# First projection half divided in the latent attention; last norm on tokens as partitions; first tail's closing norm in halves of token pairs

## The chip, the cores and the metric

The kernel runs on one core of a Trainium2 chip. The metric is the device time of one execution in microseconds. The kernel before has a median of 2648.96 us in 3 runs (2647.46 to 2650.83). One execution was profiled; it took 2648.21 us.

## What is computed

Two blocks run one after the other on one sequence of 512 tokens with 1024 features. The first block (a hybrid mixer and a mixture of experts) is not touched. The second block has two layers, each of a mixer and an MLP with residual sums and layer norms:

```python
x = layer_norm(ALPHA * x + (1 + gate_m) * (mixer(h) @ w), ln_mix_g, ln_mix_b)   # layer 0: latent attention, w = mla_w_o
h = x * (1 + scale) + shift                                              # of the next mixer or MLP
x = layer_norm(ALPHA * x + (1 + gate_f) * mlp(h), ln_ffn_g, ln_ffn_b)           # mlp: relu(h @ w1 + b1) ** 2 @ w2 + b2
```

`w1` is 1024 x 4096, `w2` 4096 x 1024. In layer 1 the mixer is S5, a state space model, whose first step is `u = h @ w_in` (1024 x 1024). The output is the x of layer 1, 512 x 1024 in f32.

## The kernel before, in words

The work is cut into stages. A stage holds one instruction stream for each engine, its instructions wait for each other by semaphores that are cleared at its start, and all engines meet between two stages. What follows a mixer in a layer is one stage, `tail_stage` (line 3734): layer 0 is **the first tail**, layer 1 **the second tail** (`last`). Before the first tail comes `latent_attention_stage` (line 3258); after it comes the stage `s5_in` (line 4995).

**Layout.** The activations are kept transposed: `k.x` is 128 partitions (features) by 8 **chunks** of 128 features by 512 tokens. A product in nearly full f32 is made of fp32r parts: ScalarE copies a tensor to its rounded **high** part (`high`), VectorE subtracts that from the tensor for the **low** part (`low`), and TensorE sums three products (high x high, high x low, low x high; `three`). To make both parts of a tensor is called **to divide** it here.

**Halves of weights.** The weights of a tail come in 36 pieces of 256 columns, called halves, numbered 0 to 35 and 1 MB each: 0 to 3 are the mixer's output projection, then come two steps with 8 halves of `w1` and 8 of `w2` each. `RES` is 4 and `EXTRA` is 5, the first two of `w1`; N is 36, so that N-2 and N-1 (34, 35) are the last two of `w2`. They give the chunks 6 and 7 of the MLP's output: 34 holds the first 1024 rows of the second step, 35 the other 1024, and both sum into the same PSUM banks. SP loads half n into one of four raw buffers once half n-4 is divided; the first four were asked for in the stage before. Each half is divided as a whole (128 x 2048) into one of two buffers; RES and EXTRA go to a free half of `big`. The order in which halves are divided is `ORDER`. A half is 2 output chunks x 8 input chunks x 3 products = 48 products of 512 columns. TensorE also runs **filler products** (`k.fill`) on unused data.

**The inner norm** of a tail (`HalvedNorm`, line 3609) follows the projection. VectorE **evicts** each output chunk from PSUM into `k.x` (`evict`: times gate plus residual). The sum of chunks 0 and 1 goes through a product with ones, the **shift product** (`pe_shift`), which gives a first guess of the mean; it is subtracted from each chunk (`dve_shift`), ScalarE squares, VectorE sums chunks and squares, and a second product with ones, the **sums** (`pe_sums`), gives mean and variance in every partition. Half 3 and all that follows the sums run in two token halves of 256, so that TensorE makes the second token half of half 3 while the first is normalised. Then each chunk is centred, scaled, given its weights by ScalarE and divided, chunk by chunk, while TensorE already multiplies chunk after chunk with RES and EXTRA.

**The closing norm** (`TokenNorm`, line 3484) has the same steps on all 512 tokens after half 35. In the first tail its result feeds the first half of the S5 projection (`ahead`, class `S5Input`, line 4949), which TensorE runs at the end of the tail: 8 chunks x 4 values of l x 3 products, where the weight operand holds every fourth token (`x[:, a, kk, l::4]`). The projection's weights are loaded and divided in four **parts**: 0 and 1 are the first column half, 2 and 3 the second. In the second tail TensorE transposes each normalised chunk (4 transposes of 128 x 128), ScalarE copies it out of PSUM, and SP stores it (8 stores of 256 KB).

**Beside it** (`beside`), the first tail prepares S5 parameters, on ScalarE and VectorE between other work; their loads are the first of the stage in SP's queue.

Of the kernel before, what the change touches and what calls it, by code (L numbers as in the profile page):

```python
# [3257 lines left out]
def latent_attention_stage(k, cq, ckv, k_pe, cos, sin, o_parts, ahead):  # L3258
# [9 lines left out]
    with k.stage("latent_attention", "w_loaded0", "w_loaded1", "qp_done", "qn_done", "kn_done", "v_done", "qn_copied", "kn_copied", "v_copied", "rope_step",  # L3268
                 "rotated", "scores_done", "masked", "max_done", "exp_done", "inverted", "probs_done", "turned", "turned_copied", "weighed", "o_high",
                 "o_low") as (block, s, sb):  # L3270
# [15 lines left out]
        def _(pe):  # L3286
# [78 lines left out]
            weigh(last - 1)  # L3365

        @block.scalar
        def _(act):
# [39 lines left out]
            for g in range(last):  # L3408
# [200 lines left out]
class HalvedNorm:  # L3609
# [10 lines left out]
    LATE_BANK = 3  # L3620

    def __init__(self, k, s, name, sq, d_sum, q_sum):
# [4 lines left out]
        self.s = {x: s[f"{name}_{x}"] for x in self.SEMS}  # L3627

# [13 lines left out]
    def pe_sums(self, pe, h):  # L3642
        s, ones, t = self.s, self.k.ones[:], token_half(h)
        pe.wait_ge(s["d_added"], self.at(KD - 1, h))
        pe.matmul(self.mean[h], ones, self.d_sum[:, t], start=True, stop=True).then_inc(s["mean_done"], 1)
        pe.wait_ge(s["q_added"], self.at(KD - 1, h))
        pe.matmul(self.var[h], ones, self.q_sum[:, t], start=True, stop=True).then_inc(s["var_done"], 1)

    def act_square(self, act, c, h=None):
        s, t = self.s, slice(0, T) if h is None else token_half(h)  # L3650
# [3 lines left out]
        act.activation(self.sq[:, c % 2, t], self.x[:, c, t], ACT.Square).then_inc(s["squared"], 1)  # L3654

    def act_spread(self, act, h):
        s = self.s
        act.wait_ge(s["mean_done"], h + 1)
        act.activation(self.d_sum[:, token_half(h)], self.mean[h], ACT.Square, scale=1.0 / D).then_inc(s["spread"], 1)

    def act_root(self, act, h):
        s, rstd = self.s, self.q_sum[:, token_half(h)]
# [8 lines left out]
    def dve_shift(self, dve, c, h=None):  # L3671
        s, t = self.s, slice(0, T) if h is None else token_half(h)
        x = self.x[:, c, t]
        if c == 0:
            dve.wait_ge(s["shift_done"], 1)
        dve.scalar_tensor_tensor(out=x, in0=self.shift[:, t], scalar=-1.0 / self.FIRST, in1=x, op0=ALU.mult, op1=ALU.add).then_inc(s["shifted"], 1)  # L3676

    def dve_add(self, dve, c, h=None):

        s, t = self.s, slice(0, T) if h is None else token_half(h)  # L3680
        at = self.at(c, h or 0)
# [3 lines left out]
        before = self.x[:, 0, t] if c == 1 else self.d_sum[:, t]  # L3685
        dve.tensor_tensor(self.d_sum[:, t], before, self.x[:, c, t], ALU.add).then_inc(s["d_added"], 1)  # L3686

    def dve_add_square(self, dve, c, h=None):
        s, t = self.s, slice(0, T) if h is None else token_half(h)
        at = self.at(c, h or 0)  # L3690
# [3 lines left out]
        before = self.sq[:, 0, t] if c == 1 else self.q_sum[:, t]  # L3694
        dve.tensor_tensor(self.q_sum[:, t], before, self.sq[:, c % 2, t], ALU.add).then_inc(s["q_added"], 1)  # L3695

    def dve_pair(self, dve, p):

        if p == 0:
            self.dve_sum(dve)  # L3700
            return
        mine = range(0 if p == 1 else 2 * p, 2 * p + 2)
# [9 lines left out]
    def dve_centre(self, dve, c, h):  # L3712
        s, x = self.s, self.x[:, c, token_half(h)]
# [4 lines left out]
    def dve_var(self, dve, h):  # L3718
        s, t = self.s, token_half(h)
        dve.wait_ge(s["spread"], h + 1)  # L3720
        dve.wait_ge(s["var_done"], h + 1)
        dve.scalar_tensor_tensor(out=self.q_sum[:, t], in0=self.var[h], scalar=1.0 / D, in1=self.d_sum[:, t], op0=ALU.mult,
                                 op1=ALU.subtract).then_inc(s["var_ready"], 1)

    def dve_scale(self, dve, c, h):
        s, t = self.s, token_half(h)
        x = self.x[:, c, t]
# [3 lines left out]
        dve.tensor_tensor(x, x, self.q_sum[:, t], ALU.mult).then_inc(s["normed"], 1)  # L3731


def tail_stage(k, layer, w_mix, x_parts, big, divided, out=None, ahead=None, beside=None):
# [18 lines left out]
    norm_sems = [f"{a}_{x}" for a, norm in (("mix", HalvedNorm), ("ffn", TokenNorm)) for x in norm.SEMS]  # L3753
    SUMS_AT, LATE_SUMS_AT = 5, 4
    with k.stage(name, "high_done", "low_done", "tile_done", "cols_step", "x_scaled", "evicted", "h_done", "x_high", "x_low", "x_ready",
# [1397 lines left out]
```

## Time and profile before

| | |
|---|---|
| median of 3 runs | 2648.96 us |
| profiled execution | 2648.21 us, span 2646.4 us |
| mean granted TensorE clock | 0.973 |
| PE (TensorE products) | 2495.6 us, 94% of the span |
| PEld (TensorE weight loads, beside the products) | 1997.6 us, 75% |
| DVE (VectorE) | 1741.0 us, 66% |
| ACT (ScalarE) | 1149.3 us, 43% |
| POOL (GpSimd) | 63.2 us, 2% |

Times in rows count from the start of the span. A timeline row gives the start, the time from the first instruction of the group to its end, the engine, the line of the code, the operation, output and inputs with their shapes, the count, and in square brackets the idle time before it with what ended it. The latent attention ends at about 1592 us of the span, the first tail at 2038.6, and the second tail runs from about 2217 to the end.

### The profile page before, as it was taken

What the parts mean: (1) busy time and instruction counts of PE and PEld (TensorE: products, weight loads), DVE (VectorE), ACT (ScalarE), POOL (GpSimd) and SP (SyncE); (2) the same over time, 40 slices, a digit from 0 to 9 for tenths busy, and PEclk for the clock granted to TensorE, in tenths of its full rate; (3) what the DMA queues carried; (4) which work ended last, traced back from release to release, by engine and by line L of the source; (5) the groups of instructions that cost most, each with busy time, mean ns of one, the idle gap of its engine ahead of it and who ended that gap; (6) DMA issues with size and microseconds to landing.
All of it is one profiled execution on the core that took longest, in us unless ns stands there. A gap on an engine that the chain in (4) does not pass through costs nothing. (4 is left out here: it accounts for less than half of the span.)

```text
span 2646.4 us, 34407 instructions
## 1 busy us (share of the span) xinstructions
PE 2495.6 (94%) x13529; PEld 1997.6 (75%) x13529; DVE 1741.0 (66%) x2582; ACT 1149.3 (43%) x1683; POOL 63.2 (2%) x166
## 2 busy tenths in 40 slices
PE   7999999999999999899998898999999889999999
PEld 5666678777777878788875457888888877888887
DVE  4899545588775666899965566677765764732435
ACT  5444422255554225588853344622324244531323
POOL 0000000000000000100001000000000000000000
PEclk9999999999999988999999999999999899999999
DMA  7887727233335733899972213234331413233221
GB/s 264 263 286 267 250 82 283 85 104 92 84 104 176 257 78 155 341 420 421 416 277 95 62 42 104 80 120 135 112 112 62 142 64 135 82 103 96 96 80 32
DMA packets 299505, 427.49 MB, mean 162 GB/s; under 512 B 27690, under 2 KB 213533, under 8 KB 289488
## 3 DMA queue, kind: packets, MB, share of 16 engines
q1 hardware_dynamic: 289424, 395.13, 43.3%
q0 software_dynamic: 5392, 20.97, 2.0%
q10 hardware_dynamic: 4528, 9.18, 0.9%
q8 instruction: 108, 1.77, 0.3%
q14 instruction: 53, 0.43, 0.0%
HBM read 384.11 MB, written 41.14 MB: 161 GB/s over the span
## 5 line engine op out<-in xcount | busy, mean ns | idle before, releaser
L3864 PE MATMUL banks<-big,late_parts 128*128 128x512 f32 (+1 forms) x2016 | 445.6, 383 | 5.9 <-PEq L151 3.8
L3864 PEld LDWEIGHTS banks<-big,late_parts 128*128 128x128 f32 x2016 | 369.5, 190 | 80.8 <-issue 6.1
L3864 PE MATMUL banks<-h_parts_second,late_parts 128*128 128x512 f32 x1344 | 305.3, 389 | 0.0
L3864 PEld LDWEIGHTS banks<-h_parts_second,late_parts 128*128 128x128 f32 x1344 | 252.2, 188 | 52.2
L4080 DVE TENSOR_TENSOR late_parts<-w_second,late_parts 128x2048 fp32r<-128x2048 f32 x67 | 153.5, 2292 | 193.1 <-ACT late_parts L3948 193.0
L2379 DVE TENSOR_TENSOR expert_parts<-w,expert_parts 128x2048 fp32r<-128x2048 f32 x102 | 232.6, 2288 | 21.7 <-ACT expert_parts L2375 20.7
L3948 ACT ACTIVATE late_parts<-w_second 128x2048 fp32r<-128x2048 f32 x67 | 128.2, 1914 | 241.8 <-PE banks L3864 241.7
L1344 PE MATMUL banks<-h_parts,ssm_parts 128*128 128x512 f32 x960 | 231.3, 398 | 0.8 <-DVE ssm_parts L1611 0.4
L2375 ACT ACTIVATE expert_parts<-w 128x2048 fp32r<-128x2048 f32 x102 | 194.7, 1916 | 60.8 <-PE banks L2386 54.2
L1344 PEld LDWEIGHTS banks<-h_parts,ssm_parts 128*128 128x128 f32 x960 | 180.3, 190 | 44.1 <-issue 6.9
L2386 PE MATMUL banks<-expert_parts,expert_xt 128*128 128x512 f32 x816 | 192.2, 395 | 4.1 <-DVE expert_xt L2367 4.1
L2386 PEld LDWEIGHTS banks<-expert_parts,expert_xt 128*128 128x128 f32 x816 | 153.5, 190 | 36.7 <-DVE expert_xt L2367 4.8
L881 PE MATMUL banks<-h_parts,front_parts 128*128 128x512 f32 x552 | 137.8, 400 | 0.0
L551 PE MATMUL banks<-h_parts,front_parts 128*128 128x512 f32 x576 | 132.2, 391 | 2.7 <-PEq L151 2.7
L551 PEld LDWEIGHTS banks<-h_parts,front_parts 128*128 128x128 f32 x576 | 108.0, 188 | 26.4 <-issue 4.2
L3982 ACT ACTIVATE tail_r<-banks,cols 128x512 f32<-128x512 f32 x64 | 40.5, 685 | 183.3 <-PE banks L3864 183.3
L551 PE MATMUL banks<-h_parts,ssm_parts 128*128 128x512 f32 x480 | 111.5, 394 | 5.9 <-DVE h_parts L1965 3.1
L881 PEld LDWEIGHTS banks<-h_parts,front_parts 128*128 128x128 f32 x552 | 101.7, 191 | 19.7
L1134 DVE SCALAR_TENSOR_TENSOR attention_mod_sum<-w,silu_c,attention_mod_sum 128x512 f32<-128x512 f32 x147 | 110.4, 751 | 4.5
L551 PEld LDWEIGHTS banks<-h_parts,ssm_parts 128*128 128x128 f32 x480 | 91.0, 190 | 26.1 <-issue 3.9
L4160 DVE TENSOR_TENSOR tail_q<-tail_r 128x512 f32<-128x512 f32 x64 | 41.4, 688 | 97.2 <-ACT tail_r L3982 97.1
L2386 PE MATMUL banks<-expert_parts,expert_ht 128*128 128x512 f32 x408 | 98.9, 399 | 3.0 <-ACT experts_y L2879 3.0
(726 smaller groups left out, 3914.1 us busy)
## 6 DMA issues: line engine op xcount, KB each, us to landing
w_second<-in_mlp_w_dram SPq DMA_DIRECT2D x64, 1024.0 KB, 5.1
w<-in_w_exp_gate_dram SPq DMA_DIRECT2D x34, 1024.0 KB, 9.0
w<-in_w_exp_up_dram SPq DMA_DIRECT2D x34, 1024.0 KB, 8.6
w<-in_w_exp_down_dram SPq DMA_DIRECT2D x34, 1024.0 KB, 8.8
w<-in_w_in_dram SPq DMA_DIRECT2D x64, 512.0 KB, 4.5
w<-in_mod_mix_w_dram SPq DMA_DIRECT2D x24, 1024.0 KB, 5.1
w<-in_mod_ffn_w_dram SPq DMA_DIRECT2D x23, 1024.0 KB, 6.1
w<-in_w_in_dram SPq DMA_DIRECT2D x16, 1024.0 KB, 5.5
```

Source lines behind the costliest of these rows:

```text
L551: mm = pe.matmul(out, self.parts[:, n % 2, w, kk, f * P:(f + 1) * P], x[:, v, kk, :], start=(start and kk == 0 and j == 0), stop=(stop and ...
L881: mm = pe.matmul(ps[:, bank, :], parts[:, j, w, kk, :], k.hp[:, x, kk, :], start=(kk == 0 and n == 0), stop=(kk == KD - 1 and n == 2))
L1134: ins = dve.scalar_tensor_tensor(out=acc, in0=w, scalar=by, in1=acc, op0=ALU.mult, op1=ALU.add)
L1344: mm = pe.matmul(ps[:, t % 2, :], parts[:, t % SPLITS, w, kk, :], k.hp[:, x, kk, :], start=(kk == 0 and j == 0), stop=(kk == KD - 1 and j ...
L2375: act.activation(self.high_part(h), self.raw(h), ACT.Copy).then_inc(self.high_done, 1)
L2379: dve.tensor_tensor(self.low_part(h), self.raw(h), self.high_part(h).bitcast(F32), ALU.subtract).then_inc(self.low_done, 1)
L2386: mm = pe.matmul(out, x[:, v, first + kk, :], self.tile(h, w, kk), start=(start and kk == 0 and j == 0), stop=(stop and kk == KE - 1 and j ...
L3864: mm = pe.matmul(ps[:, bank(n, f), t] if out is None else out, w_part(n, w)[:, kk, f * P:(f + 1) * P], x[:, v, kk, t], start=(first_chunk( ...
L3948: act.activation(w_part(n, 0), raw_half(k, n), ACT.Copy).then_inc(s["high_done"], 1)
L3982: act.activation(r[:, c % 2, :], ps[:, bank(n, c % HT), :], ACT.Relu, bias=k.cols[:, b1 + at:b1 + at + 1]).then_inc(s["relu_done"], 1)
L4080: dve.tensor_tensor(w_part(n, 1), raw_half(k, n), w_part(n, 0).bitcast(F32), ALU.subtract).then_inc(s["low_done"], 1)
L4160: dve.tensor_tensor(q[:, c % 2, :], r[:, c % 2, :], r[:, c % 2, :], ALU.mult).then_inc(s["squared"], 1)
```

## The change

It has three parts.

**Projection and inner norm.** Half 0 of `mla_w_o` is divided in the latent attention stage (ScalarE and VectorE, between the heads' last steps) into a free part of `big`; the filler products move from the start of the first tail to the end of the attention's TensorE stream. In the first tail `ORDER` becomes 0, 1, 2, RES, EXTRA, 3. In both tails the shift product stands between the two output chunks of half 1, the weight copy of half 6 two chunks later, and VectorE's order around it is new.

**Closing norm of the first tail** (`PairedNorm`). Halves 34 and 35 and all that follows are run in two halves of tokens, each of which holds two neighbouring tokens of every four (256 columns as 128 pairs). The S5 projection starts with l = 0 and 1 on the first half. Part 1 of its weights is divided by GpSimd instead of VectorE.

**Closing norm of the second tail** (`ClosingNorm`). Halves 34 and 35 run in two token halves. TensorE transposes the shifted chunks between the products of these halves, and ScalarE copies them to `by_token` (tokens as partitions). The sums are products with a single column of ones, so that mean and deviation are one number per partition. Two VectorE operations on 128 x 1024 finish a block of 128 tokens (`weigh`, `finish`); for block 0 GpSimd does the second. Four stores of 512 KB follow. The rows of weight and bias of the norm are loaded to all partitions at the start of the stage, ahead of the weights in SP's queue.

```diff
+            k.fill(pe, ps[:, 7, 0:P], 14)
...
+                if g == last - 4:
+                    act.wait_ge(k.raw_loaded[0], 16 * (k.raw_base[0] + 1))
+                    act.activation(room[0], raw_half(k, 0), ACT.Copy).then_inc(s["w_high"], 1)
...
+                if g + 2 == last:
+                    dve.wait_ge(s["w_high"], 1)
+                    dve.tensor_tensor(room[1], raw_half(k, 0), room[0].bitcast(F32), ALU.subtract).then_inc(s["w_low"], 1)
...
+class PairedNorm(HalvedNorm):
...
+    SPREAD_AFTER = "var_done"
...
+    def pick(self, ap, h):
+        if h is None:
+            return ap
+        return ap.rearrange("p (j l) -> p j l", l=S5_HALF)[:, :, h * (S5_HALF // 2):(h + 1) * (S5_HALF // 2)]
...
+class ClosingNorm(HalvedNorm):
...
+    def pe_sums(self, pe, h):
+        s, one = self.s, self.k.ones[:, 0:1]
+        for which, (total, added, done) in enumerate(((self.d_sum, "d_added", "mean_done"), (self.q_sum, "q_added", "var_done"))):
+            pe.wait_ge(s[added], self.at(KD - 1, h))
+            for j in range(self.BLOCKS):
+                b = h * self.BLOCKS + j
+                mm = pe.matmul(self.sums_of(h, which)[:, j:j + 1], total[:, b * P:(b + 1) * P], one, start=True, stop=True)
+            mm.then_inc(s[done], 1)
...
+    def dve_stats(self, dve, h, step):
+        s, b = self.s, self.blocks(h)
+        dve.wait_ge(s["mean_done"], h + 1)
+        dve.wait_ge(s["var_done"], h + 1)
+        step(dve.tensor_scalar(self.stats[:, 0, b], self.sums_of(h, 0), 1.0 / D, None, ALU.mult))
+        step(dve.tensor_tensor(self.stats[:, 1, b], self.stats[:, 0, b], self.stats[:, 0, b], ALU.mult))
+        dve.scalar_tensor_tensor(out=self.stats[:, 2, b], in0=self.sums_of(h, 1), scalar=1.0 / D, in1=self.stats[:, 1, b], op0=ALU.mult,
+                                 op1=ALU.subtract).then_inc(s["var_ready"], 1)
...
-        ORDER = (0, 1, RES, EXTRA, 2, 3, *range(EXTRA + 1, N))
+        extra = [half_room(big, j) for j in range(2)]
...
+        ORDER = (0, 1, *((RES, EXTRA, 2) if last else (2, RES, EXTRA)), 3, *range(EXTRA + 1, N))
...
+        in_extra = {RES: 0, EXTRA: 1} if last else {0: 0, RES: 1, EXTRA: 0}
...
+            if last:
+                for j, row in enumerate(("ln_ffn_g_2", "ln_ffn_b_2")):
+                    sp.dma_start(out_rows[:, j, :], k.ins[row][layer:layer + 1, :].to_broadcast([P, D])).then_inc(s["rows_loaded"], 16)
...
+                for b in range(TB):
+                    if b == 0:
+                        sp.wait_ge(s["out_pool"], 2)
+                    else:
+                        sp.wait_ge(s["out_ready"], b)
+                    sp.dma_start(out[0, b * P:(b + 1) * P, :], y[:, b, :]).then_inc(s["stored"], 16)
+                sp.wait_ge(s["stored"], 16 * TB)
...
+                pool.wait_ge(s["next_high"], 2)
+                ahead.low(pool, 1, s["next_pool"])
+            else:
+                pool.wait_ge(s["weighed"], 1)
+                pool.wait_ge(ffn_norm.s["root_done"], 1)
+                pool.tensor_scalar(y[:, 0, :], y[:, 0, :], ffn_norm.scalar(2, 0), None, ALU.mult).then_inc(s["out_pool"], 1)
+                pool.wait_ge(s["out_pool"], 1)
+                pool.tensor_tensor(y[:, 0, :], y[:, 0, :], out_rows[:, 1, :], ALU.add).then_inc(s["out_pool"], 1)
...
-            if not split:
-                k.fill(pe, ps[:, 0, 0:P], 14)
+                    if f == 0 and between is not None:
+                        between(pe)
...
+            def closing_products(n, x):
+                pe.wait_ge(s["low_done"], place[n] + 1)
+                final = n == N - 1
+                for h in range(2):
+                    for f in range(HT):
+                        if n == N - 2 and h == 1:
+                            pe.wait_ge(s["added"], KD + (4 + 2 * f if last else 4))
+                        for kk in range(KD):
+                            mm = three(n, f, kk, x, ffn_norm.late(KD - 2 + f, h), lambda ap: ffn_norm.pick(ap, h))
+                            if final and h == 1 and f == 0 and kk == SUMS_AT:
+                                if last:
+                                    for c in (KD - 2, KD - 1):
+                                        ffn_norm.pe_turn(pe, c, s["turned"], s["out_copied"], 0)
+                                ffn_norm.pe_sums(pe, 0)
+                        if h == 1:
+                            mm.then_inc(s["tile_done"], 1)
+                        elif final:
+                            mm.then_inc(ffn_norm.s["early_done"], 1)
+                        if last and n == N - 2:
+                            for c in ((0, 1), (2,), (3, 4), (5,))[2 * h + f]:
+                                ffn_norm.pe_turn(pe, c, s["turned"], s["out_copied"])
...
+                products(n, x_parts, between=mix_norm.pe_shift if n == 1 else None)
...
+                pe.wait_ge(s["next_low"], 1)
+                for h in range(2):
+                    for kk in range(KD):
+                        if h == 0 and kk == ahead.HK:
+                            pe.wait_ge(s["next_pool"], 1)
+                        pe.wait_ge(s["x_low"], 2 * KD + KD * h + kk + 1)
+                        for l in range(h * (S5_HALF // 2), (h + 1) * (S5_HALF // 2)):
+                            ahead.products(pe, 0, l, kk)
+                        if h == 0 and kk == LATE_SUMS_AT:
+                            ffn_norm.pe_sums(pe, 1)
...
+            for j in range(2, 6):
+                high(ORDER[j])
+                if j >= 4:
+                    mix_norm.act_square(act, 2 * (j - 4))
+                    mix_norm.act_square(act, 2 * (j - 4) + 1)
...
+            halves_to_parts(mix_norm, H_SCALE, 0, lambda: high(EXTRA + 1))
...
+                            ffn_norm.act_square(act, c)
+                elif last and n == N - 2:
+                    for c in range(KD - 2):
+                        ffn_norm.act_copy(act, c, s["turned"], s["out_copied"])
...
-                turned_out(KD - 1)
+                for h in range(2):
+                    for c in (KD - 2, KD - 1):
+                        ffn_norm.act_square(act, c, h)
+                    for c in (KD - 2, KD - 1):
+                        ffn_norm.act_copy(act, c, s["turned"], s["out_copied"], h)
+                    ffn_norm.act_root(act, h)
...
+            def close():
+                closing = Steps(dve, s["closing_step"])
+                dve.wait_ge(s["rows_loaded"], 32)
+                for c in (KD - 2, KD - 1):
+                    add_and_sum(c, 0)
+                ffn_norm.dve_stats(dve, 0, closing)
+                weigh(0)
+                weigh(1)
+                add_and_sum(KD - 2, 1)
+                add_and_sum(KD - 1, 1)
+                finish(1)
+                ffn_norm.dve_stats(dve, 1, closing)
+                weigh(2)
+                weigh(3)
+                finish(2)
+                finish(3)
...
+            dve.sem_inc(s["low_done"], 1)
...
                 for c in range(2 * n, 2 * n + 2):
...
-                        evict_half(c, 0)
-                        mix_norm.dve_add(dve, c, 0)
-                        mix_norm.dve_add_square(dve, c, 0)
-                if n < RES - 1:
-                    mix_norm.dve_pair(dve, n)
-            normalise_halves()
+                    evict(c)
+                if n == 0:
+                    mix_norm.dve_sum(dve)
+                if n < 2:
+                    low(ORDER[4 + n])
+                mix_norm.dve_pair(dve, n)
...
+                        else:
+                            dve.wait_ge(s["next_high"], 1)
+                            ahead.low(dve, 0, s["next_low"])
+                            for c in (KD - 2, KD - 1):
+                                add_and_sum(c, 0)
+                            beside.beside(n)
+                            normalise_halves(ffn_norm, 2 * KD, add_half)
```

## Rows read from the trace of the kernel before

**Rows 1.** windows: busy us (instructions) by engine, clock, DMA; second tail's start and middle
```profile
2217.00:2242.00 25.00, 24.18 (x96) 19.81 (x97) 11.68 (x8) 14.44 (x13) 1.49 (x7) 0.88 0.40 126
...
2300.00:2400.00 100.00, 100.00 (x443) 82.84 (x442) 41.72 (x40) 38.29 (x44) 0.00 (x0) 1.00 0.30 96
```

**Rows 2.** timeline: start, us, engine, line, idle before; end of attention, start of first tail
```profile
1591.04 0.69 DVE L3449 CAST big<-banks 128x512 fp32r<-128x512 f32 x1 [2.59 <-PE banks L3338]
...
1592.78 3.36 PE L158 MATMUL banks<-ident 128*128 128x128 f32 x28 [1.77 <-PEq L151]
...
1598.33 23.64 PE L3864 MATMUL banks<-big,late_parts 128*128 128x512 f32 x96 [2.19 <-DVE late_parts L4080]
...
1600.26 84.25 SPq L3819 DMA_DIRECT2D w_second<-in_mlp_w_dram  x8
...
1606.83 1.92 ACT L3948 ACTIVATE big<-w_second 128x2048 fp32r<-128x2048 f32 x1 [4.92 <-DMA w_second<-in_mlp_w_dram]
```

**Rows 3.** timeline: first tail's inner norm and the products behind it
```profile
1644.01 0.70 PE L3645 MATMUL banks<-tail_sums,ones 128*128 128x256 f32 x2 [2.34 <-DVE tail_sums L3686]
...
1648.89 6.30 PE L3864 MATMUL banks<-h_parts_second,big 128*128 128x256 f32 x48 [0.16 <-DVE h_parts_second L4102]
...
1671.04 2.28 DVE L4080 TENSOR_TENSOR late_parts<-w_second,late_parts 128x2048 fp32r<-128x2048 f32 x1
```

**Rows 4.** timeline: second tail's start, inner norm and the products behind it
```profile
2217.82 24.54 PE L3864 MATMUL banks<-big,late_parts 128*128 128x512 f32 x96 [3.76 <-PEq L151]
...
2237.29 0.69 DVE L3669 TENSOR_TENSOR tail_sums<-x 128x512 f32<-128x512 f32 x1
...
2264.39 1.22 PE L3645 MATMUL banks<-tail_sums,ones 128*128 128x256 f32 x2 [2.34 <-DVE tail_sums L3686]
...
2270.40 7.64 PE L3864 MATMUL banks<-h_parts_second,big 128*128 128x256 f32 x60
...
2287.36 8.90 PE L3864 MATMUL banks<-h_parts_second,big 128*128 128x256 f32 x72 [0.55 <-DVE h_parts_second L4102]
```

**Rows 5.** timeline: first tail's last halves, its closing norm, the next stage
```profile
1980.97 1.92 ACT L3948 ACTIVATE late_parts<-w_second 128x2048 fp32r<-128x2048 f32 x1 [8.54 <-PE banks L3864]
...
2014.16 24.45 PE L4978 MATMUL banks<-big,h_parts_second 128*128 128x512 f32 x96 [2.36 <-DVE h_parts_second L4151]
...
2025.80 4.49 DVE L4987 TENSOR_TENSOR big<-w_second,big 128x2048 fp32r<-128x2048 f32 x2 [1.12 <-ACT big L4984]
...
2038.91 2.54 PE L4473 MATMUL banks<-ident,w_second 128*64 128x128 f32 x32 [0.30 <-PEq L151]
```

**Rows 6.** timeline: second tail's last halves and closing transposes
```profile
2601.94 1.92 ACT L3948 ACTIVATE late_parts<-w_second 128x2048 fp32r<-128x2048 f32 x1 [8.62 <-PE banks L3864]
...
2633.55 0.42 PEld L3939 LDWEIGHTS banks<-ident,x 128*128 128x128 f32 x4 [0.97 <-ACT x L4059]
```

**Rows 7.** timeline: a GpSimd addition beside a VectorE one
```profile
744.51 1.29 POOL L1330 TENSOR_TENSOR ssm_sq<-ssm_sq 128x512 f32<-128x512 f32 x1 [61.12 <-ACT ssm_sq L1545]
...
744.67 1.55 DVE L1715 TENSOR_TENSOR x<-x,ssm_parts_plain 128x384 f32<-128x384 f32 x1
```

**Rows 8.** lines by form, 1650 to 2647 us: busy us, mean ns, idle before
```profile
L3864 PEld LDWEIGHTS banks<-h_parts_second,late_parts 128*128 128x128 f32 x1344 | 252.2, 188 | 52.2
...
L4978 PEld LDWEIGHTS banks<-big,h_parts_second 128*128 128x128 f32 x192 | 46.1, 311 | 3.4 <-issue 2.7
...
L4742 ACT ACTIVATE h_parts_second_plain<-banks 128x256 f32<-128x256 f32 x16 | 8.2, 673 | 2.0 <-PE banks L4671 2.0
...
L3731 DVE TENSOR_TENSOR x<-x,tail_sums 128x256 f32<-128x256 f32 x29 | 12.1, 418 | 0.1
...
L4639 PEld LDWEIGHTS banks<-x,big_plain 64*64 64x64 f32 x384 | 11.5, 133 | 2.0 <-issue 1.0 <-ACT x L4722 1.0
...
L4656 PEld LDWEIGHTS banks<-big_plain,x 64*64 64x64 f32 x96 | 5.9, 136 | 0.2 <-issue 0.2
```

**Rows 9.** DMA issues: size of each, median us to landing
```profile
s_rotations<-s_room SPq DMA_DIRECT2D x4, 512.0 KB, 3.0
```

More of the change, by code:

```diff
@@ L3255, in width, with half_room, latent_attention_stage @@
         return (g % TB + 1) * P
-def latent_attention_stage(k, cq, ckv, k_pe, cos, sin, o_parts, ahead):
+def half_room(big, j):
+    return [big[:, v, KD + j * KD // 2:KD + (j + 1) * KD // 2, :].rearrange("p c t -> p (c t)").rearrange("p (k n) -> p k n", k=KD) for v in range(2)]
+def latent_attention_stage(k, cq, ckv, k_pe, cos, sin, o_parts, ahead, room):
     ps = k.ps
@@ L3620 @@
     LATE_BANK = 3
+    SPREAD_AFTER = "mean_done"
     def __init__(self, k, s, name, sq, d_sum, q_sum):
@@ L3770, in tail_stage @@
             k.raw_base[slot] += N // 4
-        split = 1 if last else 0
         b1 = k.places["mlp_b1_2"][0] + layer * K2
@@ L3789, in w_part, with used_before @@
         def w_part(n, j):
-            if n in (RES, EXTRA):
-                return extra[n - RES][:, j].rearrange("p c t -> p (c t)").rearrange("p (k n) -> p k n", k=KD)
-            return parts[:, n % 2, j]
+            kind, slot = room_of(n)
+            return extra[slot][j] if kind == "extra" else parts[:, slot, j]
+        def used_before(n):
+            return max((m for m in range(n) if room_of(m) == room_of(n)), default=None)
         def bank(n, f):
@@ L3872, in last_chunk, with products @@
                 return n < RES + UP or of(n)[1] < UP or (of(n)[1] - UP) % 2 == 1
-            def products(n, x):
-                if n >= split:
+            def products(n, x, between=None):
+                if n >= 1:
                     pe.wait_ge(s["low_done"], place[n] + 1)
@@ L3920, in _ @@
                     pe.wait_ge(s["relu_done"], HK * i + HT * (g + 5))
+                    if n >= N - 2:
+                        closing_products(n, hidden[:, :, chunk * KD:(chunk + 1) * KD, :])
+                        continue
                     products(n, hidden[:, :, chunk * KD:(chunk + 1) * KD, :])
@@ L3968, in half_affine, with halves_to_parts @@
                 act.wait_ge(s["h_done"], i + 1)
-                act.activation(h_parts[:, 0, c, t], q_half(i), ACT.Copy).then_inc(s["x_high"], 1)
+                act.activation(norm.pick(h_parts[:, 0, c], h), q_half(norm, i), ACT.Copy).then_inc(s["x_high"], 1)
+            def halves_to_parts(norm, at, before, between):
+                for c in (KD - 2, KD - 1):
+                    norm.act_square(act, c, 0)
+                norm.act_spread(act, 0)
+                norm.act_root(act, 0)
+                for c in range(KD):
+                    half_affine(c, 0, norm, at, before)
+                    if c == 4:
+                        norm.act_square(act, KD - 2, 1)
+                        norm.act_square(act, KD - 1, 1)
+                    if c == 6:
+                        norm.act_spread(act, 1)
+                norm.act_root(act, 1)
+                for c in range(KD):
+                    half_affine(c, 1, norm, at, before)
+                    if c == 3:
+                        between()
@@ L4131, in normalise_halves @@
                     if c >= 1:
-                        half_low(c - 1, 1)
-                half_low(KD - 1, 1)
+                        half_low(c - 1, 1, norm, before)
+                half_low(KD - 1, 1, norm, before)
             def add(n):
```

348 lines of the change are left out of this document (169 added, 179 removed).

## The prediction

> **What bounds the kernel now.** I read the page's busy times first (in the table above): TensorE is busy nearly all the span. The windows say what that means inside a tail: in 100 us of its middle TensorE has no free time, 443 products of 512 columns at full clock, 0.2257 us each [rows 1]. So nothing that VectorE, ScalarE or the queues do there is worth anything; the change can only give or take time where TensorE stands, and costs where it gives TensorE more to do. I then read the timeline at the four places the diff touches. The reader is to see four gaps. At the start of the first tail TensorE waits from 1591.04 to 1598.33 [rows 2]. In the inner norm of each tail it stands 2.34 us for the sums [rows 3, 4]. Between the first tail's last half and the S5 projection lies some 11 us: halves 34 and 35 begin at 1980.9 (when ScalarE sees half 33 done) and need 96 x 0.2257 = 21.7 us, to 2002.6; the projection's first product starts at 2014.16 [rows 5]. After the last product of the second tail comes a closing chain of VectorE, ScalarE, transposes and stores: from half 33's end (2601.9) [rows 6] to the span's end, 2646.4, are 44.5 us, of which 21.7 are products.
>
> After a gap TensorE also runs slower for a while: the 96 products behind the 3.76 us gap took 24.54 us instead of 21.67 [rows 4], in a stretch whose mean granted clock is 0.88, so part of it at 1.2 instead of 2.4 GHz [rows 1]. The same 96 cost 23.64 behind 2.19 us of idle [rows 2] and 24.45 behind 2.36 us [rows 5]. I price a gap above 2 us at 2.0 to 2.9 us on top of itself.
>
> **Term 1, start and inner norm of the first tail.** Half 0 of the projection is divided in the attention stage; its VectorE subtraction (2.25 us, half of 4.49 [rows 5]) fits the 2.59 us for which VectorE waits there anyway [rows 2], the ScalarE copy lies in similar waits. If that cover were gone, the hand-over would slip by up to 2.25 us. But the filler products (3.36 us) now stand ahead of the stage's end instead of behind it. A stage begins 0.30 us after its last engine ended (2014.16 + 24.45 = 2038.61, next 2038.91 [rows 5]), so the tail begins at 1591.04 + 3.36 + 0.30 = 1594.7, not 1592.78; products start 3.6 us earlier than 1598.33.
> This does not last. The shift product now stands in the middle of half 1, after 72 products, at 1594.7 + 16.25 = 1610.95. It needs the sum of two evicted chunks, and VectorE evicts only after dividing halves 1, 2 and 4 (`for n in ORDER[1:4]: low(n)`). Half 4's load is queued on SP behind the S5 parameter loads, 7.5 us after the stage began, and ScalarE's copy waited for it until 1606.83, 14.05 us after [rows 2]. Again 14.05 us: 1608.75; copy 1.92, subtraction 2.25, two evictions and a sum, about 0.7 each: 1615.0. So TensorE stands 4.1 us at a place where it did not stand before; behind the waiting product are queued the second chunk of half 1 and halves 2 and 3, and VectorE's eviction of chunk 3 waits for these. Half 4's load no longer waits for half 0's subtraction, but SP is not free sooner. With 0.9 for the shift and 24 products (5.4), half 1 ends at 1621.4, plus 2.0 to 2.9 for the clock, say 1623.8; before, 1598.33 + 23.64 + 0.9 = 1622.9. The early start is lost: 0.9 us later.
> Then the reordering pays: chunk 0 and 1 are shifted, summed and squared before half 1 ends. Counting VectorE's operations from there (half 3's subtraction, chunks 2 to 5, two half chunks) the sums are ready 19.3 us after it, about when TensorE arrives; before they were ready after 21.1 (1644.01 - 1622.9) [rows 3]. Gain 1.8. The weight copy that stood between the second and third chunk of the second token half moves two chunks on and its 0.55 us stall (seen in the twin [rows 4]) goes. Term 1: -0.9 + 1.8 + 0.55 = 1.5 gained. Bounds: -0.5 (the clock lost for longer) and 3.9 (clock kept).
>
> **Term 2, inner norm of the second tail.** Here halves 4 and 5 come in time: the sum began at 2237.29 and was ready at 2238.0 [rows 4], behind the subtractions of four halves; half 2's (2.25) now stands behind it, so 2235.7, and TensorE arrives at 2236.9 (2217.82 + 24.54 - 5.4) [rows 4]. No stall. The same 1.8 to 2.0 us, and the slow clock behind the stall (6.0 us from the sums to the products at 2270.40 against 4.9 in the twin, 1644.01 to 1648.89 [rows 3, 4]), 1.1, and 0.55: 3.5 us. Two broadcast row loads now stand ahead of the weights on SP; at worst they cost the 1.2 us of slack and a stall. I take 3.3, bounds 1.4 and 3.6.
>
> **Term 3, the first tail's closing norm.** Halves 34 and 35 run as 256 columns: 192 products instead of 96. 48 took 6.30 us, 72 took 8.90 [rows 3, 4]: 0.131 and 0.124, I take 0.127. Half 34: 12.2 instead of 10.8. ScalarE divides two S5 parts after it (3.8 us), VectorE the first of them, to 16.6 (all from 1980.9), and GpSimd the second, 128 x 2048. GpSimd's 128 x 512 addition took 1.29 us; four times that is 5.2, to 21.8. Beside that addition a VectorE operation on 384 columns took 1.55 us and ended when GpSimd's end (745.80) had left it its own 0.4 [rows 7]: an operation that reads two SBUF tensors waits for GpSimd. The sums of the first late chunk are such, so they wait to 21.8. (The Trainium skill, GPSIMD Engine Reference, section Elementwise — side-by-side cycle accounting, gives 4.50 us for an addition of this size; by that the term would be 0.7 us better.) With the second chunk (four operations of about 0.42 [rows 8], plus one left of the first) the sums are complete at 24.2, not at 20.8 where TensorE arrives. From the sums to the last subtraction of the normalised chunks the inner norm took 1644.01 to 1671.04, less 1.92 for the copy in it, 25.1 us [rows 3]; 0.6 more since the square now waits for the variance product. Then two more copies and two subtractions of S5 weights, which were hidden before, 6.4 us (1.9 + 4.49 [rows 5]): 56.3. TensorE's 96 products end about 2 us before that, so VectorE ends the stage; TensorE's new wait for GpSimd's half of the weights falls at about 35 and is long met. Before: 2038.61 - 1980.9 = 57.7. Term 3: 1.4 gained. Without GpSimd's hold, 3.2 more: 4.6. Dearer pair operands on ScalarE: a copy that writes every eighth element took 0.67 us for 256 [rows 8] against about 0.4; were half of that 0.27 paid on pairs, 32 operations would cost some 3.2 us: -1.8.
>
> **How pairs of tokens are read.** A weight load that takes every fourth element took 311 ns against 188 packed; one that takes every second, 136 against 133 [rows 8]. So I price pairs (two of four) at nothing on TensorE. The Trainium skill, Advanced Engine Details and Errata (section SBUF Cachelines), says both that two accesses to a 16-byte line are enough to hide the memory's latency and that a new line at each access costs something; by the first clause the sum stands, by a charge for each new line it would move towards rival 1. The row at every second element bears out the first; no row shows the moving operand in pairs.
>
> **Term 4, the second tail's closing norm.** From 2601.9 [rows 6]: half 34 12.2, six chunks of four transposes at 0.105 [rows 6] 2.5, a wait of 1.4 for ScalarE's first copy (it comes after half 35's copy and subtraction, two additions, a shift and two squares, at 7.7, and takes 0.6; TensorE is there at 7.0): 16.1. Half 35 to the sums: 48 + 18 products, 8.4, transposes and sums 1.4: 25.9. Three small operations, then two 128 x 1024 operations of 1.2 (between 0.42 for 256 and 2.25 for 2048 columns [rows 5, 8]): 29.0. GpSimd's block 0, 1.1 + 2.6, holds up the sums of the last two half chunks as in term 3: 35.0, not 32.6. Then 1.2, sums and scalars 0.5, four operations of 1.16: 41.4. The last store is now 512 KB, like one that took 3.0 [rows 9], and 0.3 for the end: 44.7 against 44.5. Term 4: -0.2. Bounds: 2.2 (GpSimd not in the way) and -1.5 (half of the remaining waits between engines longer).
>
> **Sum.** 1.5 + 3.3 + 1.4 - 0.2 = 6.0 us off the profiled execution's 2648.21 (1.8 around its span): 2642.2. That execution is 0.75 below the median, 2648.96; I put the time between both levels, **2642.5 us**.
>
> **Rivals.** (1) Slower: pairs are dear as TensorE's moving operand. Place: the 192 products of term 3. From 32 ns more each the whole gain is gone (6.0 / 192). At half of the 311 - 188 = 123 ns per 128 columns, over 256 columns 123 ns, it is 23.6 us: 2666. For it: the 311. Against: the 136. (2) GpSimd holds nothing up: 3.2 + 2.4 more gained, 2636.9. Against it stands the 1.55 us. (3) No stall at the moved shift, or the clock kept: 2.4 more, 2640.1; it needs half 4's load earlier, which nothing brings. (4) Pairs dear on ScalarE and VectorE alone: 2645.7.
>
> **How the numbers follow.** Forecast 0.50, rival 1 0.07, 2 0.15, 3 0.10, 4 0.18. A measurement of this kernel can tell about 0.2%, 5.3 us: faster means under 2643.7. The forecast, with about 2.5 us either way, lies there for two thirds, rivals 2 and 3 wholly, 4 for a tenth: 0.57. Slower (over 2654.3) is rival 1 and a rest of mishaps: 0.09. Same: 0.34. The range goes from 2636 (rival 2) to 2654, which leaves rival 1 out.
>
> **What would show it.** Right: TensorE idle about 4 us in the middle of half 1 of the first tail, no idle before the inner sums of either, VectorE operations beside GpSimd's 128 x 2048 one stretched, VectorE last before the S5 stage. Wrong: 256-column products above 0.15 us in half 34 of the first tail (rival 1); GpSimd's operation over before 2000 or VectorE unhindered beside it (rival 2); half 1 without a gap (rival 3); ScalarE's operations on 256 columns in pairs above 0.5 (copy) and 0.7 us (rival 4).

## The result, and the profile after

The changed kernel is slower by 0.3%: median 2656.56 us in 11 runs against 2648.04 us in 11, ratio 1.0028, 95% interval 1.0017 to 1.0038. Forecast were 2642.5 us and a range of 2636 to 2654.

The two profiles (spans 2646.4 and 2654.3 us) are compared stretch by stretch. The first fence shows the ends of stretches in the kernel before that no group above has; the second the timeline of the changed kernel, first tail (columns as in the rows above).

```profile
1675.14 45.07 PE L3864 MATMUL banks<-h_parts_second,late_parts 128*128 128x512 f32 x198
...
2296.10 24.22 PE L3864 MATMUL banks<-h_parts_second,late_parts 128*128 128x512 f32 x106
```

```profile
1592.53 0.69 DVE L3458 CAST big<-banks 128x512 fp32r<-128x512 f32 x1 [0.39 <-PE banks L3343]
...
1595.92 11.16 PE L4008 MATMUL banks<-big 128*128 128x512 f32 x48 [0.30 <-PEq L151]
1606.92 5.60 PE L4008 MATMUL banks<-big,late_parts 128*128 128x512 f32 x24
...
1611.28 1.91 ACT L4113 ACTIVATE big<-w_second 128x2048 fp32r<-128x2048 f32 x1 [6.21 <-DMA w_second<-in_mlp_w_dram]
...
1617.74 2.08 PE L3657 MATMUL banks<-tail_sums,ones 128*128 128x512 f32 x2 [5.22 <-DVE tail_sums L3686]
...
1644.99 0.70 PE L3662 MATMUL banks<-tail_sums,ones 128*128 128x256 f32 x2 [0.24 <-DVE tail_sums L3701]
...
1674.90 45.30 PE L4008 MATMUL banks<-h_parts_second,late_parts 128*128 128x512 f32 x199
...
1980.73 1.91 ACT L4113 ACTIVATE late_parts<-w_second 128x2048 fp32r<-128x2048 f32 x1 [8.96 <-PE banks L4008]
...
2006.62 4.86 POOL L5169 TENSOR_TENSOR big<-w_second,big 128x2048 fp32r<-128x2048 f32 x1 [405.11 <-ACT big L5166]
...
2009.25 2.52 DVE L3701 TENSOR_TENSOR tail_sums<-tail_sums,x 128x256 f32<-128x256 f32 x1
...
2017.71 0.63 PE L3662 MATMUL banks<-tail_sums,ones 128*128 128x256 f32 x2
...
2051.95 2.54 PE L4655 MATMUL banks<-ident,w_second 128*64 128x128 f32 x32 [1.37 <-PEq L151]
```

The reader is to see the new wait of 5.22 us at the moved shift product, almost none before the inner sums, and at the end no wait at all before the sums at 2017.71, though they come 37.0 us after half 33's end (1980.73, where ScalarE, which waits for that half, starts its next copy): TensorE was busy all that time. The second tail of the changed kernel:

```profile
2230.34 19.02 PE L4008 MATMUL banks<-big,late_parts 128*128 128x512 f32 x72 [3.76 <-PEq L151]
2249.66 1.12 PE L3657 MATMUL banks<-tail_sums,ones 128*128 128x512 f32 x2 [0.29 <-DVE tail_sums L3686]
...
2305.20 15.15 PE L4008 MATMUL banks<-h_parts_second,late_parts 128*128 128x512 f32 x66
...
2611.04 1.91 ACT L4113 ACTIVATE late_parts<-w_second 128x2048 fp32r<-128x2048 f32 x1 [8.96 <-PE banks L4008]
...
2638.18 3.75 POOL L4000 TENSOR_SCALAR h_parts_second_plain<-h_parts_second_plain,tail_stats 128x1024 f32<-128x1024 f32 x1 [405.86 <-DVE h_parts_second_plain L4316]
...
2640.54 0.42 DVE L3709 TENSOR_TENSOR tail_sums<-tail_sums,tail_r 128x256 f32<-128x256 f32 x1
...
2642.01 2.47 POOL L4002 TENSOR_TENSOR h_parts_second_plain<-h_parts_second_plain,tail_out_rows 128x1024 f32<-128x1024 f32 x1
...
2642.30 2.46 DVE L3709 TENSOR_TENSOR tail_sums<-tail_sums,tail_r 128x256 f32<-128x256 f32 x1
```

From such rows, with [rows 2, 4, 5, 6] for before:

| stretch | before | after | gained | forecast |
|---|---|---|---|---|
| span's start to the last head's cast (1591.04, 1592.53) | 1591.04 | 1592.53 | -1.49 | 0 (half 0's division hidden) |
| to the first 512-column products of the first MLP (term 1) | 84.10 | 82.37 | 1.73 | 1.5 |
| to half 33's end | 305.83 | 305.83 | 0 | 0 |
| to the S5 stage's first product (term 3) | 57.94 | 71.22 | -13.28 | 1.4 |
| to the second tail's first product | 178.91 | 178.39 | 0.52 | not touched |
| to the first 512-column products of its MLP (term 2) | 78.28 | 74.86 | 3.42 | 3.3 |
| to half 33's end | 305.84 | 305.84 | 0 | 0 |
| to the span's end (term 4) | 44.46 | 43.26 | 1.20 | -0.2 |
| sum | 2646.4 | 2654.3 | -7.90 | |

The first stretch holds the division of half 0. It did not delay the hand-over: the last cast follows the one before it by 7.06 us in both kernels (from 1583.98 and 1585.47). The 1.49 us were lost earlier, and in the nine profiles below, whose attention stage is the same as the changed kernel's, the last cast lies anywhere from 1590.0 to 1594.5.

Terms 1, 2 and 4 came in at or above the forecast; term 3 is the loss. Its price is in the lines by form (count, busy us, mean ns of one) of the changed kernel, 1975 to 2060 us:

```profile
L4008 PE MATMUL banks<-big,late_parts 128*128 128x256 f32 x192 | 44.6, 413 | 0.0
...
L4008 PE MATMUL banks<-big,late_parts 128*128 128x512 f32 x25 | 5.8, 389 | 0.0
```

A product of 256 columns read in pairs holds TensorE for 44.6 / 192 = 0.232 us, as long as one of 512 packed columns (5.8 / 25 = 0.232). The clock is not the reason: the granted clock was 1.00 from 1981 to 2003 us (third number from the end of the row).

```profile
1981.00:2003.00 22.00, 22.00 (x98) 19.87 (x97) 7.58 (x9) 3.12 (x4) 0.00 (x0) 1.00 0.19 66
```

The second tail's 192 products of the same size read packed columns:

```profile
L4008 PE MATMUL banks<-big,late_parts 128*128 128x256 f32 x192 | 24.4, 285 | 0.0
```

That is 0.127 us each; the pairs cost 20.2 us of TensorE.

### The profile page after: what moved, and what is told of

Read it like the earlier page. It is cut to its first block and busy times, and to the rows that moved or that the text cites. A ratio compares the mean times of both kernels' runs of the same rounds, so it can differ in the third digit from the quotient of the medians.

```text
span 2654.3 us, 34754 instructions
## 1 busy us (share of the span) xinstructions
PE 2497.8 (94%) x13649; PEld 2010.7 (76%) x13649; DVE 1751.3 (66%) x2626; ACT 1149.9 (43%) x1701; POOL 74.8 (3%) x169
## 5 line engine op out<-in xcount | busy, mean ns | idle before, releaser
L4008 PE MATMUL banks<-big,late_parts 128*128 128x512 f32 (+1 forms) x2160 | 458.4, 375 | 3.8 <-PEq L151 3.8
L4008 PEld LDWEIGHTS banks<-big,late_parts 128*128 128x128 f32 x2160 | 386.7, 191 | 73.4 <-issue 6.6
L1344 PEld LDWEIGHTS banks<-h_parts,ssm_parts 128*128 128x128 f32 x960 | 178.4, 188 | 43.1 <-issue 6.5
```

The source lines that it names most:

```text
L1344: mm = pe.matmul(ps[:, t % 2, :], parts[:, t % SPLITS, w, kk, :], k.hp[:, x, kk, :], start=(kk == 0 and j == 0), stop=(kk == KD - 1 and j ...
L4008: mm = pe.matmul(pick(ps[:, bank(n, f), :]) if out is None else out, w_part(n, w)[:, kk, f * P:(f + 1) * P], pick(x[:, v, kk, :]), start=( ...
```

## The experiments

Nine kernels ran. Ratios are to the kernel before, run on the same chip. Three ran once only (eight ways to read, GpSimd out of the second tail's closing, steps of the weight operand) and are read from their profiles.

**Pair order.** The hidden activations of the first tail's second MLP step are stored with the tokens of the first half first, so that halves 34 and 35 read packed columns; VectorE puts the tokens back when it evicts.

```diff
+                    if i == STEPS - 1 and not last:
+                        dst, src = dst.rearrange("p (h j l) -> p h j l", h=2, l=2), src.rearrange("p (j h l) -> p h j l", h=2, l=2)
+                    act.activation(dst, src, ACT.Relu, ...
...
-                            mm = three(n, f, kk, x, ffn_norm.late(KD - 2 + f, h), lambda ap: ffn_norm.pick(ap, h))
+                            mm = three(n, f, kk, x, ffn_norm.late_flat(KD - 2 + f, h), lambda ap: ap[:, token_half(h)])
```

> The changed kernel, but the hidden activations of the first tail's second step are written in pair order, so that the products of halves 34 and 35 read 256 packed columns. Theory A (a product that reads its moving operand in pairs takes the time of 512 columns, 0.232 us instead of 0.127, and nothing else of part 3 is dear): the 192 products take 24.4 instead of 44.6 us; the sums then wait for VectorE behind GpSimd's subtraction, at 24.2 us after half 33's end instead of 37.0, so some 12.8 us of the 20.2 come back: ratio to the kernel before 0.998 (0.9972 to 0.9990). Theory B (pairs are dear on ScalarE and VectorE too, or the closing chain is longer for another reason): the sums come no earlier than 30 us after half 33's end, ratio above 1.000.

Measured: 2641.64 us, ratio 0.9965 (0.9952 to 0.9977). Its timeline:

```profile
1979.03 1.91 ACT L4119 ACTIVATE late_parts<-w_second 128x2048 fp32r<-128x2048 f32 x1 [8.96 <-PE banks L4014]
...
1994.35 4.84 POOL L5183 TENSOR_TENSOR big<-w_second,big 128x2048 fp32r<-128x2048 f32 x1 [394.15 <-ACT big L5180]
...
1995.15 0.42 DVE L3692 SCALAR_TENSOR_TENSOR x<-banks,x 128x256 f32<-128x256 f32 x1
1995.61 3.86 DVE L3701 TENSOR_TENSOR tail_sums<-tail_sums,x 128x256 f32<-128x256 f32 x1
...
2001.17 1.05 PE L3662 MATMUL banks<-tail_sums,ones 128*128 128x256 f32 x2 [2.81 <-DVE tail_sums L3701]
...
2034.54 2.54 PE L4669 MATMUL banks<-ident,w_second 128*64 128x128 f32 x32 [1.37 <-PEq L151]
```

The sums come 2001.17 - 1979.03 = 22.14 us after half 33's end, and the stretch of term 3 is 2034.54 - 1979.03 = 55.51 us instead of 71.22. Theory A holds, and theory B falls: with packed columns the paired norm is 2.4 us shorter than the old one, for 1.4 forecast, with GpSimd's hold and TensorE's wait for it in the trace. The ratio lies a little below A's range.

**Eight ways to read the moving operand**, in one kernel, each with a line of its own, such as

```diff
+            def every_second(n, f, kk, x, out, w, v, st, sp):
+                return pe.matmul(out, w_part(n, w)[:, kk, f * P:(f + 1) * P], x[:, v, kk, :].rearrange("p (j l) -> p j l", l=2)[:, :, 0], start=st, stop=sp)
```

> The changed kernel, with eight ways to read the moving operand in the closing products of the first tail (24 products each; other tokens than the norm's are read, so the output of chunks 6 and 7 is other than the reference's). If a product is paid by the 16-byte lines (four f32) that it reads, at 512 columns of 0.226 us in 128 lines: 256 packed columns 0.127 (64 lines), 4 of 8 aligned 0.127 (64 lines), 4 of 8 across lines 0.226 (128), 6 of 8 (252 columns, 84 lines) 0.15, 2 of 4 0.23 (128), 2 of 4 across lines 0.45 (254 lines), every second 0.23 (128 lines), every fourth (128 columns, 128 lines) 0.23. If instead any step that isn't packed halves the rate: 4 of 8 takes 0.23 like 2 of 4, every fourth 0.13, and across lines or not makes no difference.

Its timeline of TensorE; the difference of two starts over the count is the price of one:

```profile
1982.34 2.99 PE L4029 MATMUL banks<-big,late_parts 128*128 128x256 f32 x24
1985.17 5.60 PE L4032 MATMUL banks<-big,late_parts 128*128 128x256 f32 x24
1990.59 5.62 PE L4035 MATMUL banks<-big,late_parts 128*128 128x256 f32 x24
1996.03 3.06 PE L4050 MATMUL banks<-big,late_parts 128*128 128x256 f32 x24
1998.92 5.61 PE L4041 MATMUL banks<-big,late_parts 128*128 128x256 f32 x24
2004.35 5.63 PE L4044 MATMUL banks<-big,late_parts 128*128 128x254 f32 x24
2009.79 2.30 PE L4047 MATMUL banks<-big,late_parts 128*128 128x128 f32 x18
2011.91 0.63 PE L3662 MATMUL banks<-tail_sums,ones 128*128 128x256 f32 x2
...
2013.51 3.80 PE L4038 MATMUL banks<-big,late_parts 128*128 128x252 f32 x24
2017.15 8.02 PE L5192 MATMUL banks<-big,h_parts_second 128*128 128x512 f32 x30
```

In this order: 4 of 8 aligned 0.118, 4 of 8 across lines 0.226, every second 0.227, packed 0.120, 2 of 4 0.226, 2 of 4 across lines 0.227, every fourth (128 columns) 0.118, 6 of 8 (252 columns) 0.152. (By starts a product comes out a little shorter than by busy time over count, 0.226 and 0.120 for 0.232 and 0.127.) Both theories miss: the price by lines fails at 2 of 4 across lines (0.227, not 0.45) and every fourth (0.118, not 0.23), the price of any step fails at 4 of 8 aligned. One rule fits: a whole aligned group of four f32 goes at 0.46 ns a column (0.118 / 256), every other column at 0.88 to 0.89. For 6 of 8 that makes (4 x 0.46 + 2 x 0.88) / 6 x 252 = 0.151 us. Every fourth can't bear it out: its 128 columns took as long as 256 packed ones, but the 28 fillers of [rows 2], 128 packed columns each (in plain f32), took 3.36 / 28 = 0.120 us too, so 0.118 may be what a product of few columns takes anyway. The rule is read from the other seven, in one run; why the chip does so isn't shown.

**The old closing norm** in the first tail, the rest as changed:

```diff
-            ffn_norm = PairedNorm(k, s, "ffn", r, sums[:, 0, :], sums[:, 1, :])
+            ffn_norm = TokenNorm(k, s, "ffn", 4, r, sums[:, 0, :], sums[:, 1, :])
...
-                    if n >= N - 2:
+                    if n >= N - 2 and last:
```

> The changed kernel with the first tail's closing norm of the kernel before (halves 34 and 35 as products of 512 columns, norm on all tokens, both first parts of the S5 weights divided by VectorE). Theory A: the loss lies in part 3 alone, 13.3 us in the profiles; without it the time is 2643 us, ratio 0.9978 (0.9970 to 0.9986), the sum of the terms 1, 2 and 4. Theory B (the profiles mislead, the other parts gain nothing against the medians): ratio 0.9995 to 1.0005.

Measured: 2643.28 us, ratio 0.9976 (0.9966 to 0.9986). Theory A: the loss lies in "part 3", the stretch of term 3 (the second of the three parts of the change), alone, and terms 1, 2 and 4 together are worth the 6.35 us (0.24%) that the profiles say.

**Evictions first** in the first tail:

```diff
-            for n in ORDER[1:4]:
+            for n in ORDER[1:4 if last else 3]:
                 low(n)
...
                     mix_norm.dve_sum(dve)
+                    if not last:
+                        low(ORDER[3])
```

> The changed kernel, but in the first tail VectorE evicts chunks 0 and 1 and sums them before it divides half 4. Theory A (the 5.2 us stall at the moved shift product is VectorE waiting for half 4's load): the stall is gone, TensorE reaches the sums 5 to 7 us earlier and waits there up to 3 us for VectorE; 3 to 5 us faster than the changed kernel, ratio to the kernel before 1.0012 (1.0003 to 1.0020). Theory B (VectorE's work up to the sums is the bound): the wait moves to the sums whole, ratio 1.0028 as the changed kernel.

Measured: 2650.72 us, ratio 1.0004 (0.9994 to 1.0014), against 1.0028. Theory A, and more of it than expected. Its timeline of TensorE:

```profile
1597.89 11.16 PE L4008 MATMUL banks<-big 128*128 128x512 f32 x48 [0.30 <-PEq L151]
...
1614.33 1.02 PE L3657 MATMUL banks<-tail_sums,ones 128*128 128x512 f32 x2
...
1639.87 0.70 PE L3662 MATMUL banks<-tail_sums,ones 128*128 128x256 f32 x2 [0.24 <-DVE tail_sums L3701]
```

From the first product to the sums are 41.98 us, in the changed kernel 1644.99 - 1595.92 = 49.07: 7.1 us less, the wait of 5.22 and the clock behind it (granted 0.79 from 1617 to 1625 us in the changed kernel, so partly at 1.2 GHz; 1.00 here from 1614 to 1622). Nothing of it comes back at the sums. The two windows, the changed kernel's first:

```profile
1617.00:1625.00 8.00, 7.26 (x23) 5.25 (x24) 6.16 (x7) 1.23 (x2) 0.00 (x0) 0.79 0.00 1
...
1614.00:1622.00 8.00, 8.00 (x35) 6.26 (x34) 6.66 (x6) 4.19 (x5) 0.00 (x0) 1.00 0.50 177
```

**GpSimd out of the first tail's closing**, on top of pair order:

```diff
-                pool.wait_ge(s["next_high"], 2)
-                ahead.low(pool, 1, s["next_pool"])
...
+                            dve.wait_ge(s["next_high"], 2)
+                            ahead.low(dve, 1, s["next_pool"])
                             beside.beside(n)
```

> The kernel with pair order, but VectorE instead of GpSimd makes the low part of part 1 of the S5 weights, after its sums of the first half's late chunks. Theory A (GpSimd's 128 x 2048 subtraction held up VectorE's addition, 3.86 us instead of 0.42): the addition takes 0.42, TensorE waits at most 0.7 us for the sums instead of 2.81, and the S5 stage begins 53.2 us after half 33's end instead of 55.5, 2.3 us faster (ratio to the kernel before 0.9956). Theory B (the addition is slow for its own pairs): it still takes above 2 us, and the stage begins 55.5 us or more after half 33's end.

Measured: 2638.87 us, ratio 0.996 (0.9944 to 0.9975). By the medians that can't be told from pair order (0.9965); the timeline tells it:

```profile
1977.66 1.91 ACT L4117 ACTIVATE late_parts<-w_second 128x2048 fp32r<-128x2048 f32 x1 [8.96 <-PE banks L4012]
...
1994.24 0.43 DVE L3701 TENSOR_TENSOR tail_sums<-tail_sums,x 128x256 f32<-128x256 f32 x1
...
1996.83 0.62 PE L3662 MATMUL banks<-tail_sums,ones 128*128 128x256 f32 x2
...
2002.72 8.02 PE L5174 MATMUL banks<-big,h_parts_second 128*128 128x512 f32 x30 [1.22 <-DVE h_parts_second L4262]
...
2030.02 2.54 PE L4669 MATMUL banks<-ident,w_second 128*64 128x128 f32 x32 [1.36 <-PEq L151]
```

The same addition takes 0.43 us, TensorE doesn't wait for the sums (it waits 1.22 us later, for the first normalised chunk), and the stretch of term 3 is 52.36 us instead of 55.51. Theory A: GpSimd held VectorE up. (The Trainium skill, GPSIMD Engine Reference, section Key points, says that the two share their SBUF interfaces and contend where VectorE has two SBUF inputs; the 3.86 and 0.43 us agree. It was not so beside every operation of GpSimd: while it multiplied a tensor by a scalar for 3.75 us in the second tail of the changed kernel, VectorE's sums, with two SBUF inputs, took 0.42 to 0.43.)

**GpSimd out of the second tail's closing** (`finish(0)` on VectorE after `weigh(1)`):

> The changed kernel, but VectorE finishes block 0 of the output (one operation more of 1.2 us) and GpSimd does nothing in the second tail's closing. Theory A (GpSimd's 128 x 1024 addition held up VectorE's last sum, 2.46 us instead of 0.42): that sum takes 0.42, and the last store is issued 0.8 us earlier, at 2.05 saved less 1.2 added. Theory B (the hold cost nothing, since VectorE waited anyway): 1.2 us later.

In one run the last sum takes 0.42 us, and from half 33's end to the span's end are 42.88 us instead of 43.26:

```profile
2645.58 0.42 DVE L3709 TENSOR_TENSOR tail_sums<-tail_sums,tail_r 128x256 f32<-128x256 f32 x1
...
2647.59 0.16 DVE L3839 TENSOR_SCALAR tail_stats<-banks 128x2 f32<-128x2 f32 x1 [0.39 <-PE banks L3812]
```

The hold is real; only 0.4 of the 0.8 us expected shows, since VectorE now waits 0.39 us for TensorE's sums.

**All four edits:**

> The changed kernel with all four edits: pair order, VectorE's evictions before half 4 in the first tail, part 1's low part and block 0 on VectorE. If they add up, by the medians and profiles so far: 0.9965 less 0.0024, 0.0009 and 0.0003, ratio to the kernel before 0.993 (0.9915 to 0.9945). If the earlier start of the first tail is given back behind it (VectorE as the bound in both): 0.9955.

Measured: 2631.22 us, ratio 0.9929 (0.9916 to 0.9943). They add up.

**Steps of the weight operand**, for the row on which the prediction had rested:

```diff
+            elif l == 1:
+                mm = pe.matmul(out, x[:, a, kk, 0:256:2], moving, start=first, stop=final)
+            elif l == 2:
+                mm = pe.matmul(out, x[:, a, kk, 0:384:3], moving, start=first, stop=final)
```

> The changed kernel, with other steps of the weight operand in the second column half of the S5 projection (it reads other tokens there, so the output is another): every fourth as before for l = 0, every second for l = 1, every third for l = 2, packed for l = 3, each 24 loads of 128 x 128. Theory A (a weight load hides a step of two, and the moving operand does not: each has its own price): every second 190 to 200 ns like packed, and its product 0.23 us; every fourth 311. Theory B (a step of two is dear in a load of this size too, and the 136 ns row was of a smaller load that had slack): every second above 240 ns.

Its lines by form, weight loads (every fourth, third, second, packed):

```profile
L5162 PEld LDWEIGHTS banks<-big,h_parts_second 128*128 128x128 f32 x28 | 6.7, 310 | 0.0
...
L5166 PEld LDWEIGHTS banks<-big,h_parts_second 128*128 128x128 f32 x24 | 5.6, 253 | 0.2 <-issue 0.2
L5164 PEld LDWEIGHTS banks<-big,h_parts_second 128*128 128x128 f32 x24 | 4.6, 193 | 0.9
L5168 PEld LDWEIGHTS banks<-big,h_parts_second 128*128 128x128 f32 x24 | 4.5, 188 | 0.9
```

Theory A: a weight load takes a step of two for 5 ns, where the moving operand pays double. Pairs in a weight load were not measured.

**Evictions first in both tails**, on top of all four edits: `for n in ORDER[1:3]`, and `low(ORDER[3])` behind the sum in both.

> The kernel with all four edits, and VectorE's evictions before the second divided half of the MLP in the second tail as well. Theory A (in the second tail the shift product waited for the loads behind the two row loads, 1.55 us in the profile with all four edits): no wait there, 1.5 us faster, ratio to the kernel before 0.9923 (0.991 to 0.9938). Theory B: the wait moves to the sums, ratio 0.9929 as with four edits.

Measured: 2628.52 us, ratio 0.9925 (0.9911 to 0.9938), the lowest median of the nine. The wait at the second tail's shift product is gone (1.55 us in the profile with four edits); the ratio can't tell it from 0.9929.

## Why the prediction was wrong

The step that failed is the one on how pairs are read: "So I price pairs (two of four) at nothing on TensorE". It took the moving operand's price from weight loads, of which a step of two is nearly free (136 and 133 ns in [rows 8]; 193 and 188 here). The moving operand pays 0.226 instead of 0.120 us, 106 ns for each of 192 products. That is the mechanism of rival 1, named with its place (the products of halves 34 and 35) and given 0.07; its sign, 256-column products above 0.15 us, is the 0.232 above. That its size (123 ns) comes near is luck: it was half of what a weight load pays at every fourth token, another operand and another step. Its 2666 us came out too high, in part because the longer products cover what else would have stood there: 71.22 - 55.51 = 15.7 of the 20.2 us show, and the kernel with pair order has a wait of 2.81 us before the sums, and a granted clock of 0.76 from 2001 to 2008 us, that the changed kernel lacks. The clause of the Trainium skill that was weighed (Advanced Engine Details and Errata, section SBUF Cachelines) asks for at least two accesses to a 16-byte line. The prediction took two as enough; for the moving operand they are not: 2 of 4 has two to a line and took 0.226 us, against 0.120 packed.

The other steps:
- Term 1 is right in sum (1.73 for 1.5) and in mechanism: the tail begins earlier, and the moved shift product gives it back. The wait is 5.22 for 4.1, since half 4's copy came 15.4 us after the stage's first product, not 14.05.
- Term 2: 3.42 for 3.3. The 1.2 us of slack taken for the two row loads was thin: 0.29 us of wait in this profile, 1.0 to 2.0 in three others, at most 0.24 in the other five with the same order in the second tail.
- Term 3 without the pairs: 2.4 for 1.4. Without GpSimd's hold it is 57.94 - 52.36 = 5.6 for 4.6, so taking GpSimd out is worth 3.15 us, as priced (3.2).
- Term 4: 1.20 for -0.2. GpSimd's first operation took 3.75 us, not 1.1, and its second held up one sum of VectorE for 2.0 us, for the 2.4 priced. The chain ran ahead of the count at each mark: from half 33's end, blocks 0 and 1 were weighed at 28.2 us for 29.0, and the last sum was done at 33.7 for 35.0.
- Rival 2 is false: GpSimd holds VectorE up. Rival 3 didn't come, since the stall stood, but its price was too small: taking the stall away is worth 7.1 us in the profiles, not 2.4. I had let VectorE's count set the time of the sums; the 0.24 us before them in both kernels shows that VectorE follows TensorE closely there. Rival 4 is false: on pairs ScalarE's copies took 0.44 us (0.42 in the inner norm, on packed columns), and VectorE's operations 0.42:

```profile
2021.87 0.44 ACT L4124 ACTIVATE h_parts_second<-tail_q 128x256 fp32r<-128x256 f32 x1
```

The stretch between the tails, which the change doesn't touch, took 178.4 to 184.0 us in these profiles. The cause is open, and it is why single spans are not compared.

## What to carry to other kernels

Take an operand's price from rows of that operand: a step that was nearly free in a weight load halved the rate of the moving side. Where a matrix product must read scattered tokens, store the producer's output in the order in which it will be read (here one rearranged activation and one eviction in two parts), so that TensorE reads whole aligned groups of four. Work on two tensors that went to GpSimd to relieve VectorE held up VectorE's operations on two SBUF tensors until it ended; and an eviction on which TensorE waits belongs ahead of a VectorE operation that waits for a load.

## What the runs showed of the hardware

- The moving operand's columns (fp32r) took 0.46 to 0.47 ns each packed or in whole aligned groups of four f32, and 0.88 to 0.89 otherwise, whether the rest of the group was skipped or its edge crossed (seven ways of reading, one run).
- Weight loads of 128 x 128 took 188 ns packed, 193 at every second element, 253 at every third, 310 at every fourth.
- GpSimd's two-input operation of 128 x 1024 stretched a VectorE sum to 2.46 us; beside its 3.75 us operation with one tensor input, just before, VectorE's sums took 0.42 to 0.43.
- Beside GpSimd's 128 x 2048 subtraction (4.84 us) an operation of VectorE with one input in PSUM took its usual 0.42 us, and the sum behind it, with two SBUF inputs, ended 0.28 us after GpSimd.
